# First FFN step of a two-layer block started pair by pair on the modulation chunks

## The chip, the cores and the metric

The kernel runs on one core of one Trainium2 chip. The metric is the device time of one execution in microseconds (us), the median of several runs. The time before is 1221.44 us, the median of 3 runs (1220.31 to 1224.39).

## The reference, cut to what matters

```python
cond = jax.nn.silu(c)                                   # c: (1, 1024)
for l in range(2):
    mod = jnp.einsum('bd,de->be', cond, w_ada[l]) + b_ada[l]      # 1024 x 9216 weights
    sh1, sc1, g1, sh2, sc2, g2, sh3, sc3, g3 = jnp.split(mod, 9, axis=-1)
    h = rms_norm(x, norm_ffn1[l]) * (1 + sc1) + sh1               # x: (256, 1024)
    x = x + 0.5 * g1 * swiglu(h, w_gate1[l], w_up1[l], w_down1[l])   # 1024 x 2816, 2816 x 1024
    h = rms_norm(x, norm_mix[l]) * (1 + sc2) + sh2
    x = x + g2 * token_mixing(h, ...)                             # three kinds of attention
    h = rms_norm(x, norm_ffn2[l]) * (1 + sc3) + sh3
    x = x + 0.5 * g3 * swiglu(h, w_gate2[l], w_up2[l], w_down2[l])
```

All is in f32. Before the first FFN can start, `sh1` and `sc1` must be known: 1024 x 2048 of `w_ada`, 8 MB.

## The kernel before

Everything is written out by hand for each engine: which instruction follows which, and the semaphores between them. Nothing is planned by a scheduler.

**Precision.** A product of f32 values is made of three products of rounded parts: a weight block `raw` (128 x 2048, 1 MB) is turned by ScalarE into `whi` (`split_hi`, line 423) and by VectorE into `wlo = raw - whi` (`split_lo`, line 726). The activations `hTf` (K-tile by token, 128 x 8 x 256) are split in the same way into `hhi` and `hlo`.

**FFN.** `ffn` runs 11 steps of 256 hidden columns. On TensorE (`ffn_step`) a step has 48 gate matmuls, 48 up matmuls (each 128x128 by 128x256) and 24 down matmuls (128x128 by 128x512). The gate product is `by_high` (lines 1129, 1130, then 1133 with `hlo`), the up and down products are `three` (lines 1071 to 1073). VectorE's part of a step begins with `weigh_ada`: two chunks of `w_ada` (for later modulations) are summed over K with silu(c) as factors (lines 682, 684). Only then come the first half of the down block's `wlo` (line 810), the product of silu(gate) and up (815), its low part (817), the second half of `wlo` (819), and the splits of the next gate and up blocks (726). ScalarE makes silu (471), `whi` of the down block, then `guhi` (475) and the next `whi`. The weights are fetched by SyncE's queue (`fill`, line 326), in the order gate, up, down; `w_ada` by GpSimd's queue (lines 385 and 393).

**The start.** `sh1` and `sc1` are the first 2048 columns of `w_ada`, in 8 chunks of 256 columns (1 MB each): chunk m of 0 to 3 holds the shifts of K-tiles 2m and 2m+1, chunk 4+m their scales. All 8 are fetched in order. Chunks 0, 2, 4, 6 go to TensorE (`dot_chunk`, line 1089): each 128x128 piece is the stationary operand and one column of silu(c) the moving one, so that the sums come out as columns, one for each of 128 partitions. Chunks 1, 3, 5, 7 go to VectorE (`weigh_chunk`) and are closed by TensorE with ones (`sum_ada`, line 1080). The first gate and up blocks are requested when chunk 6 has landed. When all 16 columns stand in one bank, `modulation` makes the factors `modA` and `modB` (769, 771), and ScalarE and VectorE put them on while they copy the transposed x out of PSUM (460, 752). ScalarE then makes `hhi` (465) and `split_hi(1, 0)`, VectorE `split_lo(0, 0)`, `hlo` (761) and `split_lo(1, ...)`, and the gate product of step 0 starts.

**Order of the queues.** Each engine takes its instructions strictly in the order written; SyncE's and GpSimd's queues fill in theirs.

Of the kernel before, what the change touches and what calls it, by code (L numbers as in the profile page):

```python
# [15 lines left out]
P = 128  # L16
# [19 lines left out]
def build(nc, x, c, w_ada, b_ada, norm_ffn1, w_gate1, w_up1, w_down1, norm_mix, w_in, qn_a, kn_a, qn_c, kn_c,  # L36
# [36 lines left out]
    ADA_PRE = 1  # L73
# [10 lines left out]
    with ctx:  # L84
# [3 lines left out]
        def sem(name):  # L88
# [63 lines left out]
        pre_ada = [ada[:, 0:1, :, :], ada[:, 1:2, :, :]] + [heads[:, 8 * k:8 * k + 8, :].unsqueeze(1) for k in range(2)] \  # L152
            + [LGs[:, :].rearrange("p (a k n) -> p a k n", a=1, k=KT), hTf[:, :, :].unsqueeze(1)] + [ada[:, 0:1, :, :], ada[:, 1:2, :, :]]
        WEIGHED = (1, 3, 5, 7)
        pre_acc = {1: acc[:, 0:1, :], 3: acc[:, 1:2, :], 5: gate[:, 0:CW].unsqueeze(1), 7: gate[:, CW:2 * CW].unsqueeze(1)}
# [9 lines left out]
        disti, dm4, dm16, strict_i = (eb[:, k * S:(k + 1) * S].bitcast(I32) for k in range(4))  # L165
        upper_i = eb[:, 4 * S:4 * S + P].bitcast(I32)
        distf = xn[:, 0, 0:S]
        ge0 = xn[:, 0, S:2 * S]
        tmpf = xn[:, 0, 2 * S:3 * S]
        maskC = xn[:, 0, 3 * S:4 * S]  # L170
# [3 lines left out]
        GB, UB0, UB1, SB_ = PS[4], PS[5], PS[6], PS[7]  # L174
        PROJ = [PS[0], PS[1], PS[7]]
# [10 lines left out]
        pre_full = [sem(f"pre_full{m}") for m in range(6)]  # L186
# [123 lines left out]
        def _(sp):  # L310
# [40 lines left out]
            sp.wait_ge(ada_full[0], 16)  # L351
            gate_up(0, 0, 0, v_gate, v_up)
# [28 lines left out]
        def _(pool):  # L381
# [30 lines left out]
        def _(act):  # L412
# [21 lines left out]
            def boundary(l, n, x_done):  # L434
# [8 lines left out]
                if l == 0 and n == 0:  # L443
                    split_hi(0, 0)
                high_of_h(l, n)
                if l == 0 and n == 0:
                    split_hi(1, 0)
# [19 lines left out]
            def ffn_step(l, which, i, ahead, after):  # L467
# [3 lines left out]
                act.activation(silu, GB[:, :], ACT.Silu).then_inc(silu_ready, 1)  # L471
# [7 lines left out]
            def ffn(l, which, after):  # L479

                with act.Fori(0, NF - 1) as i:
# [82 lines left out]

            act.wait_ge(tables, 1)
            act.preload_act_table_set("natural_log_exp_and_others")
            for l in range(L):
                boundary(l, 0, nth(l, NB * TT, 0))
# [59 lines left out]
        def _(dve):  # L628
# [8 lines left out]
            for k in range(2):  # L637
                dve.memset(heads1[k * HD:(k + 1) * HD, k * HD:(k + 1) * HD], 1.0)
            dve.wait_ge(iotas, 3)
# [26 lines left out]
            dve.drain()  # L666
            s_a, s_c = slopes()
            for h in range(H_A):
                dve.scalar_tensor_tensor(aliA[:, h, :], distf, -s_a[h], causal[:, :], ALU.mult, ALU.add)
            for h in range(H_C):  # L670
                dve.scalar_tensor_tensor(aliC[:, h, :], distf, -s_c[h], maskC, ALU.mult, ALU.add)
            def late_tables():
                dve.wait_ge(cols_done, 1)
                dve.tensor_copy(cols[:, :, :, :], PS[0][:, 0:L * KT * 13].rearrange("p (l k m) -> p l k m", l=L, k=KT))
                dve.wait_ge(gains_in, 8 * 16)
# [13 lines left out]
            def weigh_chunk(m):  # L689

                dve.wait_ge(pre_full[m] if m < 6 else ada_full[m - 6], 16)
                weigh_rows(pre_acc[m], pre_ada[m])
                if m in (1, 7):
                    dve.drain().then_inc(ada_used[1], 1)
# [51 lines left out]
            def transposed(l, n, gain, shift):  # L746
# [9 lines left out]
                if l == 0 and n == 0:  # L756
                    split_lo(0, 0)
# [697 lines left out]
```

## Time and profile before

| | us |
|---|---|
| median of 3 runs | 1221.44 (1220.31 to 1224.39) |
| the profiled execution, its own time | 1223.01 |
| its span, first to last instruction | 1221.3 |
| TensorE busy | 1163.4 (95%) |
| VectorE busy | 873.8 (72%) |
| ScalarE busy | 530.8 (43%) |
| read from HBM | 256.56 MB, mean 211 GB/s over the span |

The profiled execution took 1223.01 us, 1.7 us more than its span and 1.6 us more than the median. TensorE is busy nearly all the time, so its busy share tells little. What matters for this change is the first 75 us, and there the time at which each piece of work starts.

In the records of the trace, one f32 matmul of the program stands as two records (a chunk's 16 matmuls are 32 records), while a matmul of split parts is one.

### The profile page before, as it was taken

The page shows a single profiled execution, that of the slowest core. Times are in us where ns is not written, and L with a number is a line of the kernel's source. Part 1 is how long each engine was busy: PE and PEld are TensorE (multiplying, and loading weights), DVE is VectorE, ACT ScalarE, POOL GpSimd, SP SyncE. Part 2 cuts the span into 40 slices and gives each one's busy share as a digit, 9 for nine tenths or more (in the row PEclk, how much of TensorE's full clock was granted, in tenths as well). Part 3 has the DMA queues.
Part 4 walks back from the last instruction along what each step waited for, and adds up shares of the span by engine and source line. Part 5 has one row for each costly group of instructions (what it writes and reads, how often), then busy time and mean ns, then how long its engine had stood idle before and what let it go on. Part 6 is the DMA issues. An engine that isn't in the chain of part 4 may idle for free.

```text
span 1221.3 us, 20469 instructions
## 1 busy us (share of the span) xinstructions
PE 1163.4 (95%) x7948; PEld 1070.2 (88%) x7948; DVE 873.8 (72%) x1304; ACT 530.8 (43%) x685; POOL 64.4 (5%) x79
## 2 busy tenths in 40 slices
PE   6899999999998889999989999999999978999998
PEld 6899999989897779999979999998989866999996
DVE  7687888876864786667678887888687577655445
ACT  2244333443566454333453344335256555334432
POOL 2011100100000000000001011100000000000000
PEclk9999999988999889999988999999899978999999
DMA  9788899934510647777756988894633044765561
GB/s 305 247 293 299 302 311 320 319 121 146 166 59 18 234 136 241 249 253 247 250 196 209 329 302 297 298 351 151 204 122 103 6 163 155 246 195 164 169 210 69
DMA packets 160209, 258.24 MB, mean 211 GB/s; under 512 B 8333, under 2 KB 127117, under 8 KB 160159
## 3 DMA queue, kind: packets, MB, share of 16 engines
q1 hardware_dynamic: 140579, 182.12, 45.3%
q0 software_dynamic: 19584, 75.50, 18.4%
q8 instruction: 29, 0.48, 0.2%
q14 instruction: 17, 0.14, 0.0%
HBM read 256.56 MB, written 1.05 MB: 211 GB/s over the span
## 4 chain that ended last, share of the span: by engine, by line
PE 85%; DVE 6%; ACT 5%; DVEq 1%; DMA 1%; issue 1%; ACTq 0%; POOL 0%; POOLq 0%
PE bank L1071 18%; PE bank L1072 18%; PE bank L1073 18%; PE bank L1129 7%; PE bank L1130 7%; PE bank L1133 7%; PE bank L1089 2%; PE bank L1330 1%; DVE wlo L726 1%; PE bank L1249 1%; ACT hhi L465 1%; DMA ada<-in_w_ada_dram 1%; PE bank L1098 1%; ACT whi L423 1%; PE bank L1234 1%
## 5 line engine op out<-in xcount | busy, mean ns | idle before, releaser
L423 ACT ACTIVATE whi<-raw 128x2048 fp32r<-128x2048 f32 (+3 forms) x178 | 323.0, 1818 | 39.8 <-DMA raw<-in_w_gate_dram 11.9
L726 DVE TENSOR_TENSOR wlo<-raw,whi 128x2048 fp32r<-128x2048 f32 (+3 forms) x134 | 283.3, 2144 | 41.9 <-ACT whi L423 40.8
L1071 PE MATMUL bank<-hhi,whi 128*128 128x256 f32 x1008 | 289.9, 288 | 0.0
L1072 PE MATMUL bank<-hlo,whi 128*128 128x256 f32 x1008 | 287.6, 285 | 0.0
L1073 PE MATMUL bank<-hhi,wlo 128*128 128x256 f32 x1008 | 287.5, 285 | 0.0
L1071 PEld LDWEIGHTS bank<-hhi,whi 128*128 128x128 f32 x1008 | 196.2, 195 | 2.3 <-issue 1.8
L1072 PEld LDWEIGHTS bank<-hlo,whi 128*128 128x128 f32 x1008 | 196.0, 194 | 0.5 <-issue 0.5
L1073 PEld LDWEIGHTS bank<-hhi,wlo 128*128 128x128 f32 x1008 | 195.9, 194 | 0.0
L471 ACT ACTIVATE eb<-bank 128x512 f32<-128x512 f32 x44 | 26.3, 597 | 367.0 <-PE bank L1133 367.0
L684 DVE SCALAR_TENSOR_TENSOR room<-ada,cT,room 128x512 f32 (+3 forms) x266 | 170.1, 639 | 20.2
L1129 PE MATMUL bank<-hhi,whi 128*128 128x256 f32 x736 | 184.4, 287 | 0.0
L1130 PE MATMUL bank<-hhi,wlo 128*128 128x256 f32 x736 | 183.8, 286 | 0.0
L810 DVE TENSOR_TENSOR wlo<-raw,whi 128x1024 fp32r<-128x1024 f32 x44 | 53.9, 1224 | 141.6 <-ACT whi L423 141.6
L1130 PEld LDWEIGHTS bank<-hhi,wlo 128*128 128x128 f32 x736 | 143.9, 195 | 1.9
L1129 PEld LDWEIGHTS bank<-hhi,whi 128*128 128x128 f32 x736 | 143.5, 195 | 2.0
L1071 PE MATMUL bank<-whi,guhi 128*128 128x512 f32 x352 | 141.0, 401 | 0.0
L1072 PE MATMUL bank<-wlo,guhi 128*128 128x512 f32 x352 | 139.2, 396 | 0.0
L1073 PE MATMUL bank<-whi,gulo 128*128 128x512 f32 x352 | 139.2, 395 | 0.0
L385 POOL DMA_DIRECT2D ada<-in_w_ada_dram x66 | 58.1, 883 | 984.0 <-DVEq L701 793.4
L1133 PE MATMUL bank<-hlo,whi 128*128 128x256 f32 x736 | 104.8, 286 | 0.0
L1133 PEld LDWEIGHTS bank<-hlo,whi 128*128 128x128 f32 x736 | 96.7, 195 | 0.0
L1073 PEld LDWEIGHTS bank<-whi,gulo 128*128 128x128 f32 x352 | 66.2, 188 | 16.1
(184 smaller groups left out, 1417.3 us busy)
## 6 DMA issues: line engine op xcount, KB each, us to landing
ada<-in_w_ada_dram POOLq DMA_DIRECT2D x68, 1024.0 KB, 5.8
raw<-in_w_gate_dram SPq DMA_DIRECT2D x44, 1024.0 KB, 5.6
raw<-in_w_up_dram SPq DMA_DIRECT2D x44, 1024.0 KB, 7.0
raw<-in_w_down_dram SPq DMA_DIRECT2D x44, 1024.0 KB, 6.5
raw<-in_w_in_dram SPq DMA_DIRECT2D x28, 1024.0 KB, 5.4
raw<-in_w_out_dram SPq DMA_DIRECT2D x8, 512.0 KB, 3.3
raw<-in_w_out_dram SPq DMA_DIRECT2D x4, 1024.0 KB, 4.8
LG<-in_b_ada_dram SPq DMA_DIRECT2D x6, 512.0 KB, 8.3
```

The lines of the kernel that those rows point to most:

```text
L385: pool.dma_start(ada[:, slot, :, :], v_ada[:, row, col]).then_inc(ada_full[slot], 16)
L423: last = act.activation(dst, src, ACT.Copy)
L471: act.activation(silu, GB[:, :], ACT.Silu).then_inc(silu_ready, 1)
L684: last = dve.scalar_tensor_tensor(sums, chunks[:, :, k, :], cT[:, k:k + 1], sums, ALU.mult, ALU.add)
L726: last = dve.tensor_tensor(dst, src, hi.bitcast(F32), ALU.subtract)
L810: dve.tensor_tensor(wlo[2][:, 0:D], raw[2][:, 0:D], whi[2][:, 0:D].bitcast(F32), ALU.subtract)
L1071: pe.matmul(ps, l_hi, r_hi, start=first, stop=False)
L1072: pe.matmul(ps, l_hi, r_lo, start=False, stop=False)
L1073: return pe.matmul(ps, l_lo, r_hi, start=False, stop=last)
L1129: pe.matmul(ps, wh[:, k, :], hhi[:, k, :], start=k == 0, stop=False)
L1130: pe.matmul(ps, wl[:, k, :], hhi[:, k, :], start=False, stop=False)
L1133: last = pe.matmul(ps, wh[:, k, :], hlo[:, k, :], start=False, stop=k == KT - 1)
```

## The change

- GpSimd fetches the 8 chunks in the order 0, 4, 1, 5, 2, 6, 3, 7. Chunk 6 waits for the dot of chunk 0, chunk 3 for that of chunk 4, and chunk 7 for VectorE's sum of chunk 1 (places in SBUF are used again).
- SyncE requests the gate block when chunk 1 (third in the order) has landed and the up block when chunk 3 (seventh) has.
- Six chunks (0, 4, 5, 6, 3, 7) are now TensorE's. In `dot_chunk` silu(c) is the stationary operand (one column), and 256 columns of the chunk stream past it, 8 f32 matmuls for a chunk. The result is a row of one partition; ScalarE copies it (`copy_row`) and TensorE turns it into columns (`turn_row`, two f32 matmuls of one column). VectorE sums chunks 1 and 2.
- The transposed x is copied out plain (ScalarE, four copies). `first_pair(p)` puts the factors of two K-tiles on it and makes `hlo` of them, `first_high(p)` makes `hhi`. `gate_pair(p)` is the quarter of the gate product of step 0 that needs these two K-tiles: 12 matmuls, with one bank for each half of the hidden columns.
- Step 0 of the first FFN is taken out of the loops of TensorE and ScalarE; VectorE's loop is as it was.
- The tables for the position biases (`aliA`, `aliC`, 12 VectorE instructions) are made at the start of token mixing in layer 0.

The core of the diff:

```diff
-            for m in range(6):
-                pool.dma_start(pre_ada[m][:, 0, :, :], v_ada[:, 0:KT, m * CW:(m + 1) * CW]).then_inc(pre_full[m], 16)
-            for k in range(2):
-                fill(k, 1, slice(0, KT), slice((6 + k) * CW, (7 + k) * CW))
+            for m in (0, 4, 1, 5, 2, 6, 3, 7):
+                if m in (6, 3):
+                    pool.wait_ge(row_done, DOTTED.index(0 if m == 6 else 4) + 1)
+                if m == 7:
+                    pool.wait_ge(pre_used, 1)
+                pool.dma_start(pre_ada[m], v_ada[:, 0:KT, m * CW:(m + 1) * CW]).then_inc(pre_full[m], 16)
...
-            sp.wait_ge(ada_full[0], 16)
-            gate_up(0, 0, 0, v_gate, v_up)
+            sp.wait_ge(pre_full[1], 16)
+            fill(0, 0, chunk_cols(raw[0]), v_gate[:, 0:KT, 0:CW])
+            sp.wait_ge(pre_full[3], 16)
+            fill(1, 0, chunk_cols(raw[1]), v_up[:, 0:KT, 0:CW])
...
+            copy_row(4)
+            copy_row(5)
+            first_high(0)
+            split_hi(0, 0)
+            first_high(1)
+            copy_row(6)
+            copy_row(3)
+            first_high(2)
+            copy_row(7)
+            first_high(3)
+            act.sem_inc(hhi_ready, TT)
+            split_hi(1, 0)
...
+            def first_pair(p):
+                ks = slice(2 * p, 2 * p + 2)
+                both = lambda a: a.rearrange("p (m k) -> p m k", m=2)
+                dve.wait_ge(sums_done, p + 1)
+                dve.tensor_tensor(both(modAB[:, :])[:, :, ks], both(PRE_SUMS[p][:, 0:4]), biasL[:, 0:2, ks], ALU.add)
+                dve.drain()
+                dve.scalar_tensor_tensor(modA[:, ks], modA[:, ks], 1.0, colL[:, ks, N_MOD], ALU.add, ALU.mult)
+                dve.drain()
+                dve.wait_ge(raw_h, 2 * TT)
+                for k in (2 * p, 2 * p + 1):
+                    last = dve.tensor_scalar(hTf[:, k, :], hTf[:, k, :], modA[:, k:k + 1], modB[:, k:k + 1], ALU.mult, op1=ALU.add)
+                last.then_inc(first_h, 1)
+                dve.wait_ge(first_hi, p + 1)
+                dve.tensor_tensor(hlo[:, ks, :], hTf[:, ks, :], hhi[:, ks, :].bitcast(F32), ALU.subtract).then_inc(first_lo, 1)
...
+            weigh_chunk(1)
+            first_pair(0)
+            split_lo(0, 0)
+            first_pair(1)
+            weigh_chunk(2)
+            first_pair(2)
+            first_pair(3)
...
             def dot_chunk(m):
+                pe.wait_ge(pre_full[m], 16)
+                n = DOTTED.index(m)
+                if n >= 2:
+                    pe.wait_ge(row_read, n - 1)
+                for k in range(KT):
+                    last = pe.matmul(PRE_ROWS[n % 2][0:1, 0:CW], cT[:, k:k + 1], pre_ada[m][:, k, :], start=k == 0, stop=k == KT - 1)
+                last.then_inc(row_done, 1)
...
+            def gate_pair(p):
+                pe.wait_ge(first_hi, p + 1)
+                if p == 0:
+                    pe.wait_ge(split_done[0], 2)
...
-            last.then_inc(modc_done, 1)
+            dot_chunk(0)
+            turn_h(0, 0)
+            dot_chunk(4)
+            turn_row(0)
+            turn_row(4).then_inc(sums_done, 1)
+            dot_chunk(5)
+            pe.wait_ge(raw_h, 2 * TT)
+            sum_ada(1, [0], PRE_SUMS[1], 0, pre_acc[1])
+            turn_row(5).then_inc(sums_done, 1)
+            gate_pair(0)
+            dot_chunk(6)
+            sum_ada(2, [0], PRE_SUMS[2], 0, pre_acc[2])
+            turn_row(6).then_inc(sums_done, 1)
+            dot_chunk(3)
+            dot_chunk(7)
+            turn_row(3)
+            turn_row(7).then_inc(sums_done, 1)
+            for p in range(1, 4):
+                last = gate_pair(p)
+            last.then_inc(g_done, 1)
```

## Rows read from the trace of the kernel before

**Rows 1.** Timeline, 0 to 75 us, TensorE: start us, us, engine, line, operation, count.
```profile
9.99 6.96 PE L1089 MATMUL bank<-cT,ada 128*128 128x1 f32 x32 [1.05 <-DMA ada<-in_w_ada_dram]
...
52.73 0.64 PE L1129 MATMUL bank<-hhi,whi 128*128 128x256 f32 x1
...
53.38 0.41 PE L1129 MATMUL bank<-hhi,whi 128*128 128x256 f32 x1
53.59 0.41 PE L1130 MATMUL bank<-hhi,wlo 128*128 128x256 f32 x1
...
59.77 1.12 PE L1133 MATMUL bank<-hlo,whi 128*128 128x256 f32 x8
60.73 0.28 PE L1071 MATMUL bank<-hhi,whi 128*128 128x256 f32 x1
...
66.48 0.40 PE L1071 MATMUL bank<-whi,guhi 128*128 128x512 f32 x1
```

**Rows 2.** Chain of waits, 0 to 75 us: start us, us, what.
```profile
2.76 11.75 DMA ada<-in_w_ada_dram
```

**Rows 3.** Issues (GpSimd at 17.25 and 19.70, SyncE at 30.51): KB each, us to landing.
```profile
ada<-in_w_ada_dram POOLq DMA_DIRECT2D x1, 1024.0 KB, 13.2
...
ada<-in_w_ada_dram POOLq DMA_DIRECT2D x1, 1024.0 KB, 13.5
...
raw<-in_w_gate_dram SPq DMA_DIRECT2D x1, 1024.0 KB, 5.7
```

**Rows 4.** Queues, whole span, then 8 to 10 and 17 to 18 us: packets, MB, share.
```profile
q1 hardware_dynamic: 140579, 182.12, 45.3%
...
q0 software_dynamic: 95, 0.39, 53.0%
q1 hardware_dynamic: 96, 0.39, 49.9%
...
q0 software_dynamic: 83, 0.34, 100.0%
q1 hardware_dynamic: 82, 0.00, 6.0%
```

**Rows 5.** Timeline, 36 to 66 us, ScalarE and VectorE.
```profile
36.25 1.91 ACT L423 ACTIVATE whi<-raw 128x2048 fp32r<-128x2048 f32 x1 [11.95 <-DMA raw<-in_w_gate_dram]
...
46.88 0.18 DVE L769 TENSOR_TENSOR modAB<-bank,biasL 128x16 f32<-128x16 f32 x1 [8.55 <-PE bank L1080]
...
48.91 1.06 ACT L465 ACTIVATE hhi<-hTf 128x1024 fp32r<-128x1024 f32 x1
...
54.44 2.28 DVE L726 TENSOR_TENSOR wlo<-raw,whi 128x2048 fp32r<-128x2048 f32 x1
...
57.20 5.71 DVE L684 SCALAR_TENSOR_TENSOR room<-ada,cT,room 128x512 f32 x7
...
63.36 1.23 DVE L810 TENSOR_TENSOR wlo<-raw,whi 128x1024 fp32r<-128x1024 f32 x1 [0.45 <-ACT whi L423]
...
65.40 0.43 DVE L817 TENSOR_TENSOR gulo<-eb,guhi 128x256 fp32r<-128x256 f32 x1 [0.49 <-ACT guhi L475]
```

**Rows 6.** Timeline, TensorE's f32 matmuls at 256 and 370 us.
```profile
256.03 2.73 PE L1098 MATMUL bank<-ones,room 128*128 128x1 f32 x24
...
370.63 0.59 PE L1295 MATMUL bank<-eb,ones 128*128 128x256 f32 x2
371.06 1.02 PE L1296 MATMUL bank<-eb,upper 128*128 128x512 f32 x2
```

**Rows 7.** Busy time by stretch: us, PE, PEld, DVE, ACT, POOL, PEclk, DMA share, GB/s.
```profile
254.00:256.00 2.00, 2.00 (x4) 0.80 (x3) 1.83 (x4) 1.93 (x6) 0.00 (x0) 0.61 0.00 0
...
260.00:262.00 2.00, 2.00 (x11) 2.00 (x11) 2.00 (x6) 0.00 (x0) 0.00 (x0) 0.50 0.33 55
```

**Rows 8.** Timeline, VectorE: the second bias table, and early token mixing.
```profile
10.74 2.76 DVE L671 SCALAR_TENSOR_TENSOR aliC<-xn 128x256 f32<-128x256 f32 x8
...
268.59 2.29 DVE L726 TENSOR_TENSOR wlo<-raw,whi 128x2048 fp32r<-128x2048 f32 x1 [5.92 <-ACT whi L423]
```

More of the change, by code:

```diff
@@ L150, in build @@
         GATE_BIAS = (0, 1, 0)
[L152 to L155, printed above, removed]
+        pre_heads = [heads[:, 8 * k:8 * k + 8, :] for k in range(2)]
+        pre_ada = {0: ada[:, 0, :, :], 4: ada[:, 1, :, :], 1: pre_heads[0], 5: pre_heads[1],
+                   2: LGs[:, :].rearrange("p (k n) -> p k n", k=KT), 6: ada[:, 0, :, :], 3: ada[:, 1, :, :], 7: pre_heads[0]}
+        WEIGHED = (1, 2)
+        DOTTED = (0, 4, 5, 6, 3, 7)
+        pre_acc = {1: acc[:, 0:1, :], 2: acc[:, 1:2, :]}
+        pre_row = lambda m: eb[0:1, 4 * S + DOTTED.index(m) % 2 * CW:4 * S + (DOTTED.index(m) % 2 + 1) * CW]
         rows = vs[0:N_MOD + 4, :, :]
@@ L183, in build @@
         ada_full = [sem(f"ada_full{k}") for k in range(2)]
-        pre_full = [sem(f"pre_full{m}") for m in range(6)]
+        pre_full = {m: sem(f"pre_full{m}") for m in pre_ada}
+        pre_used = sem("pre_used")
+        row_done = sem("row_done")
+        row_read = sem("row_read")
+        raw_h = sem("raw_h")
+        sums_done = sem("sums_done")
+        first_h = sem("first_h")
+        first_hi = sem("first_hi")
+        first_lo = sem("first_lo")
+        gate_first = sem("gate_first")
         ada_used = [sem(f"ada_used{k}") for k in range(2)]
@@ L465, in high_of_h, with ffn_step @@
                     act.activation(hhi[:, :, t * P:(t + 1) * P], hTf[:, :, t * P:(t + 1) * P], ACT.Copy).then_inc(hhi_ready, 1)
-            def ffn_step(l, which, i, ahead, after):
+            def ffn_step(l, which, i, ahead, after, gated=False):
                 base = turn(l, U_FFN[which])
@@ L479, in ffn @@
             def ffn(l, which, after):
-                with act.Fori(0, NF - 1) as i:
+                if l == 0 and which == 0:
+                    ffn_step(l, which, 0, True, turn(l, U_FFN[which] + 1), True)
+                with act.Fori(1 if l == 0 and which == 0 else 0, NF - 1) as i:
                     ffn_step(l, which, i, True, turn(l, U_FFN[which] + 1))
@@ L665, in _, with alibi @@
                 dve.tensor_tensor(maskC, maskC, ge0, ALU.add)
[L666 to L671, printed above, removed]
+            def alibi(which):
+                s_a, s_c = slopes()
+                if which == 0:
+                    for h in range(H_A):
+                        dve.scalar_tensor_tensor(aliA[:, h, :], distf, -s_a[h], causal[:, :], ALU.mult, ALU.add)
+                else:
+                    for h in range(H_C):
+                        dve.scalar_tensor_tensor(aliC[:, h, :], distf, -s_c[h], maskC, ALU.mult, ALU.add)
             def late_tables():
@@ L755, in transposed @@
                     last.then_inc(hTf_ready, 1)
-                if l == 0 and n == 0:
-                    split_lo(0, 0)
                 for t in range(TT):
@@ L982, in _ @@
                         head_norm(l, n - 2)
+                    if l == 0 and n in (0, 1):
+                        alibi(n)
                     if n + 2 < NC:
@@ L1134, in by_high, with ffn_step @@
                 return last
[L1136 removed]
+            def ffn_step(l, which, i, is_last, gated=False):
                 use = i + turn(l, U_FFN[which])
                 n = i + nth(l, 2 * NF, which * NF)
[L1139 to L1143 removed]
+                if not gated:
+                    pe.wait_ge(split_done[0], use + 2)
+                    wh, wl = chunk_cols(whi[0]), chunk_cols(wlo[0])
+                    for ft in range(2):
+                        last = by_high(l, 2 * which, GB[:, ft * S:(ft + 1) * S], wh[:, :, ft * P:(ft + 1) * P], wl[:, :, ft * P:(ft + 1) * P])
+                    last.then_inc(g_done, 1)
                 pe.wait_ge(split_done[1], use + 2)
@@ L1187, in ffn @@
                     pe.matmul(DB[b][:, :], zero16[:, :], zero16[:, :].unsqueeze(1).to_broadcast([P, HALF // P, P]), start=True, stop=False)
-                with pe.Fori(0, NF - 1) as i:
+                if l == 0 and which == 0:
+                    ffn_step(l, which, 0, False, True)
+                with pe.Fori(1 if l == 0 and which == 0 else 0, NF - 1) as i:
                     ffn_step(l, which, i, False)
```

130 lines of the change are left out of this document (73 added, 57 removed).

## Prediction

> **What bounds the kernel now.** I read the page first, for the share of TensorE; then the chain of waits over 0 to 75 us; then the timelines of that stretch, engine by engine; then the landing of each transfer and what each queue moved. The kernel is TensorE's from the first gate matmul on: it starts at 52.73, the gate product ends and the up product starts at 60.73, and the first down matmul starts at 66.48, with no wait between [rows 1]. So the change is worth what it moves that down matmul, as long as the later steps follow one another as before.
>
> Ahead of 52.73 the chain is first a transfer (the second chunk, landed at 2.76 + 11.75 = 14.5 [rows 2]) and then TensorE's own column sums: 6.96 us a chunk [rows 1]. The transfers were done sooner: chunks 6 and 7 landed at 17.25 + 13.2 = 30.5 and 19.70 + 13.5 = 33.2, the gate block at 30.51 + 5.7 = 36.2 [rows 3]. That is (33.2 - 14.5) / 6 = 3.1 us for each MB, the wires being full.
>
> TensorE's clock has to be read from spacings here. Early matmuls 256 columns wide start 0.21 us apart (53.38, 53.59), later ones (1.12 - 0.28) / 7 = 0.12 us [rows 1]: 1.2 and 2.4 GHz. The one-column records start (6.96 - 0.35) / 31 = 0.21 us apart early and (2.73 - 0.25) / 23 = 0.11 us at 256 us [rows 1, 6]. So TensorE, though busy, ran at 1.2 GHz until some 5 us after 52.73.
>
> **Part 1, the dots.** A chunk is now 8 f32 matmuls of 256 columns, two records each. Two such records take 371.06 - 370.63 = 0.43 us at 2.4 GHz [rows 6], so a chunk takes 8 x 0.43 = 3.4 us, and at 1.2 GHz 6.9 us, which is what it takes now. All depends on the clock. For 2.4 GHz speaks that wide f32 matmuls (L1106) brought it up by 256 us (0.61 granted over 254 to 256 [rows 7]); against it that 27 us of one-column products did not. With one stationary column nothing in the trace shows it. I take the wide moving operand as the nearer likeness: 2.4 GHz from about 15 us.
> The Trainium skill, "TensorE: Matmul & The Clock Gate", section "Part 1: The HAM clock gate", says that the throttled state is the default and that activity releases it. The early row does not agree if activity means a busy engine: busy with one-column products it stayed at 1.2 GHz. By the rule the dots cost 3.4 us; by that row 6.9.
>
> **Part 2, TensorE until it must wait.** Dot 0 from 9.99, up to 15 at 1.2 GHz (0.73 of it) and the rest at 2.4: 15.9. The transposes wait for x and VectorE; I put their end at 19.6. Dot 4 ends at 23.0; two turns of rows (two one-column matmuls each, 0.22 us apiece) and a ScalarE copy of some 0.5 (between 0.18 and 1.06 [rows 5]) end at 24.2; dot 5 at 27.6; closing chunk 1's sum and a turn, 28.6. Next in TensorE's order is `gate_pair(0)`, and behind it stand dots 6, 3, 7 and all the other pairs.
>
> **Part 3, the new wait.** `gate_pair(0)` needs the gate block, landed and split. It is requested at the landing of the third chunk, 14.5 + 3.1 = 17.6 (some 18), instead of 30.51. But GpSimd's queue is then full of chunks, and the engines serve the two queues packet by packet: 95 against 96 packets over 8 to 10 us, and 83 against 82 over 17 to 18 us, where one side moved 0.34 MB and the other 0.00 [rows 4]. GpSimd's packets hold 0.39 MB / 95 = 4.1 KB, SyncE's on the whole 182.12 MB / 140579 = 1.3 KB, and those of a block with rows of 1 KB, 1 KB. So the gate block gets one byte in five, about 0.07 of 0.34 MB/us, from 20 us on: 20 + 1.05 / 0.07 = 35. It lands at 35.3, against 36.2 before. This is where the head start goes. Then 1.91 and 2.28 us for its two splits [rows 5] and 0.2 between them: `gate_pair(0)` starts at 39.7, after a wait of 11 us. VectorE's sum of chunk 1 and its other work before this are over by 25 and hide there; ScalarE's are too.
>
> **Part 4, what is queued behind it.** After the wait the clock is 1.2 GHz again, for up to 5 us (as after 52.73). Pair 0: 12 x 0.21 = 2.6, to 42.3. Dot 6: 0.35 of it by 44.7, the rest at 2.4 GHz, 46.9. Sum and turn of chunks 2 and 6 (VectorE's sum of chunk 2 after `first_pair(1)` is ready at about 46.6), 1.2: 48.1. Dots 3 and 7, whose chunks have landed by 37: 6.9, to 55.0. Two turns and a copy, 1.3: the last sums stand at **S = 56.3**. Pairs 1 to 3: 36 x 0.12 = 4.3, gate product done at 60.6. So far it is as before (60.73).
>
> **Part 5, what is late next.** The up product waits for two splits that before were done by 56.7 (54.44 + 2.28 [rows 5]). Now ScalarE's `split_hi(1, 0)` stands behind `first_high(3)`, which stands behind S. From S: two small operations and two multiplications on VectorE 1.2 (from 0.18 and the like), `first_high` 0.6 (half of 1.06), 1.9, 2.3 [rows 5], 0.1: the up product starts at S + 6.1 = 62.4. Behind that same `split_lo` VectorE has, as always, `weigh_ada` ahead of the down block: from 56.64 (0.47, then 5.71 from 57.20) to 62.9, then 63.36 to the end of the first `gulo` at 65.83 [rows 5]. That is 6.3 + 2.5 = 8.8 us that was hidden under 60.73 to 66.48 and now starts at 62.4: the first down matmul at S + 14.9 = **71.2**, against 66.48: 4.7 us later. The next gate block's split follows 2.3 us after the second `gulo`, still under the 5.6 us of down products, so step 1 goes on without a further wait. Between up and down TensorE now waits 3 us; should the clock fall there, as it did after 2.73 us of one-column work at 256 us (granted 0.50 over 260 to 262 [rows 6, 7]), that costs 0 to 1.7 us more.
>
> **Parts at nothing.** The bias tables (2.76 us for eight instructions, so 4.2 for twelve) move into early token mixing, where VectorE waits 5.92 us at once for ScalarE [rows 8]; without that gap they would cost the 4.2. The loops shortened by one step, and the added semaphores, I put at 0, between -0.5 and +0.5.
>
> **Sum.** +4.7 and some 0.3 for the possible fall of the clock: +5.0 on 1223.01, 1228.0 for a profiled execution. That one was 1.6 above the median, so the median is 1221.4 + 5.0 = **1226.4**; with the bounds, 1224.5 to 1229.
>
> **Rivals.** (a) *The clock stays low through the dots.* For it: 27 us of one-column products, and one stationary column is little work; against it: wide f32 matmuls raised it. Dot 0 to 17, transposes 20.5, dot 4 27.4, dot 5 36, pair 0 from 41.4 to 44, dots 6, 3, 7 with sums: S = 44 + 3 x 6.9 + 3 = 67.7. The down matmul comes at S + 14.9 = 82.6: +16, **1237.5**. It decides as soon as a dot takes over some 4 us.
> (b) *The gate block is early.* Were the queues served byte for byte, or SyncE first, it would land at 20 + 6.3 = 26.5; then `split_hi(0, 0)` follows the copy of row 5 and `gate_pair(0)` starts at 32.7, 7 us sooner; chunk 7 lands at 38. S = 48.5 to 49.3, down at 63.3 to 64.2: -2.3 to -3.2, **1218.5**. Against it: [rows 4]. The Trainium skill, "DMA: Bandwidth & Descriptors", section "Queues, rings and completion order", says that an engine takes whole packets from the queues in turn; the trace agrees (95 to 96), and it is against this change.
> (c) *The clock does not fall in the wait, or is back at once*: pair 0 and dot 6 save 1.1 + 1.2, **1224**.
> (d) *A cheaper start than I count* (an engine order that overlaps more, the 8.8 us of VectorE shorter), no mechanism seen: below 1218.
>
> **How the numbers follow.** Forecast 0.50 (1224.5 to 1229), (a) 0.22, (b) 0.12, (c) 0.10, (d) 0.06. 0.3% is 3.7 us, about what can be told from no change. Faster: (d) and half of (b), 0.12. Same: half of (b), most of (c), a little of the forecast's lower end: 0.19. Slower: 0.69. The range 1218 to 1238 takes in all but (d), the lower half of (b) and the upper part of (a).
>
> **What would show it.** The gate block's landing near 35; dots of 3.4 us after the first; a wait of some 11 us before `gate_pair(0)`; up from 62 and down from 71; VectorE's `weigh_ada` starting only with the up product. It is wrong if dots take 6.9 us, if the gate block lands before 30, or if the down product starts before 67.

## The result

The median of five runs of the changed kernel is 1231.3 us (1227.16 to 1235.62), against 1221.44 for the kernel before in the same round: a ratio of 1.0061, with a 95% interval of 1.0032 to 1.0091. It is slower by 7.5 us by the ratio and by 9.9 us by the medians; another round (experiment 12, below) gave 1236.24 us and 1.0109. The forecast was 1226.4 (1224.5 to 1229 if its mechanism held), with a range of 1218 to 1238 over all rivals and "slower" the likeliest. The profiled execution took 1233.36 us with a span of 1231.7, against 1223.01 and 1221.3: 10.4 more. So it shows the loss, and can be read against the kernel before.

The first fence is the TensorE timeline of the changed kernel up to the second step (start, duration, engine and line, operands, count, and in brackets the idle time before it with what ended it). It answers to [rows 1].

```profile
9.91 6.07 PE L1169 MATMUL bank<-ada,cT 128*1 128x256 f32 x16 [0.74 <-DMA ada<-in_w_ada_dram]
...
20.15 3.61 PE L1169 MATMUL bank<-ada,cT 128*1 128x256 f32 x16
...
24.76 3.61 PE L1169 MATMUL bank<-room,cT 128*1 128x256 f32 x16
...
28.84 0.60 PE L1178 MATMUL bank<-ones,eb 1*128 1x1 f32 x4
39.33 0.55 PE L1196 MATMUL bank<-hhi,whi 128*128 128x256 f32 x1 [9.89 <-DVE wlo L800]
...
42.16 3.63 PE L1169 MATMUL bank<-ada,cT 128*1 128x256 f32 x16
...
54.01 1.13 PE L1178 MATMUL bank<-ones,eb 1*128 1x1 f32 x8
55.07 0.39 PE L1196 MATMUL bank<-hhi,whi 128*128 128x256 f32 x1
...
61.25 0.39 PE L1149 MATMUL bank<-hhi,whi 128*128 128x256 f32 x1 [0.72 <-DVE wlo L800]
...
70.14 0.80 PE L1149 MATMUL bank<-whi,guhi 128*128 128x512 f32 x1 [2.88 <-DVE gulo L886]
70.73 0.63 PE L1150 MATMUL bank<-wlo,guhi 128*128 128x512 f32 x1
71.16 0.63 PE L1151 MATMUL bank<-whi,gulo 128*128 128x512 f32 x1
...
76.79 0.40 PE L1150 MATMUL bank<-wlo,guhi 128*128 128x512 f32 x1
77.03 0.40 PE L1151 MATMUL bank<-whi,gulo 128*128 128x512 f32 x1
...
78.66 0.28 PE L1235 MATMUL bank<-hhi,whi 128*128 128x256 f32 x1
```

A chunk's dots take 3.61 us, half of the 6.96 of [rows 1], and the engine still gains nothing, since it then waits 9.89 us for the gate block. The last sums stand at S = 55.1 and the first down matmul starts at 70.14, against 66.48. The down matmuls then start 0.43 us apart (70.73, 71.16) instead of 0.24 (76.79, 77.03, which is the spacing of the kernel before too) until 76.3. The second step's gate product starts at 78.66, against 72.09 before: 6.6 us later.

The second fence is ScalarE and VectorE over the same stretch, which answers to [rows 5].

```profile
34.95 1.91 ACT L439 ACTIVATE whi<-raw 128x2048 fp32r<-128x2048 f32 x1 [5.65 <-DMA raw<-in_w_gate_dram]
36.89 2.29 DVE L800 TENSOR_TENSOR wlo<-raw,whi 128x2048 fp32r<-128x2048 f32 x1 [6.87 <-ACT whi L439]
...
56.97 1.90 ACT L439 ACTIVATE whi<-raw 128x2048 fp32r<-128x2048 f32 x1
58.90 2.29 DVE L800 TENSOR_TENSOR wlo<-raw,whi 128x2048 fp32r<-128x2048 f32 x1 [1.03 <-ACT whi L439]
61.67 5.72 DVE L742 SCALAR_TENSOR_TENSOR room<-ada,cT,room 128x512 f32 x7
...
69.66 0.42 DVE L886 TENSOR_TENSOR gulo<-eb,guhi 128x256 fp32r<-128x256 f32 x1 [0.48 <-ACT guhi L491]
```

The up block's splits run at 56.97 and 58.90, behind S. `weigh_ada` runs behind them, from 61.11 to 67.4, and `gulo` at 69.66 lets the down product go.

The table shows how much later than in the kernel before ScalarE's `silu` comes in its one profiled execution. It comes once in every FFN step, so it tells in which stage time is lost. In these three nothing changes within the first FFN; nearly all that changes does so between FFNs (boundaries and token mixing).

| us against the kernel before | second step | end of FFN 1 | after mixing, layer 0 | before mixing, layer 1 | after it |
|---|---|---|---|---|---|
| changed kernel | +6.58 | +6.58 | +7.15 | +5.90 | +10.30 |
| changed kernel, once more | +4.20 | +4.20 | +8.44 | +8.46 | +12.05 |
| kernel before, once more | -0.10 | -0.10 | -0.15 | -0.15 | -0.12 |

In the first profile two thirds of the loss are made in the first 78 us. Behind them 3.7 us more appear: +0.6 in layer 0's mixing, -1.3 from there to layer 1's, and +4.4 in layer 1's mixing. The second profile of the same kernel has other parts: 4.2, then 4.2 and 3.6 in the two mixings. So a difference of 2 us between two single profiles, at any of these places, is not yet an effect.

### The profile page after: what moved, and what is told of

Its sections match the earlier page's. It is cut to its first block, busy times and chain, and to the rows that moved or that the text cites. A ratio compares the mean times of both kernels' runs of the same rounds, so it can differ in the third digit from the quotient of the medians.

```text
span 1231.7 us, 20425 instructions
## 1 busy us (share of the span) xinstructions
PE 1163.1 (94%) x7932; PEld 1053.3 (86%) x7932; DVE 867.9 (70%) x1296; ACT 532.2 (43%) x690; POOL 64.6 (5%) x79
## 4 chain that ended last, share of the span: by engine, by line
PE 76%; DVE 10%; ACT 5%; DMA 4%; DVEq 2%; issue 2%; ACTq 0%; POOL 0%; POOLq 0%
PE bank L1149 17%; PE bank L1150 17%; PE bank L1151 17%; PE bank L1236 6%; PE bank L1239 6%; PE bank L1235 6%; DVE room L742 2%; DVE wlo L800 2%; DMA ada<-in_w_ada_dram 2%; DMA raw<-in_w_gate_dram 1%; PE bank L1439 1%; PE bank L1358 1%; DMA room<-in_w_ada_dram 1%; ACT whi L439 1%; ACT hhi L477 1%
## 5 line engine op out<-in xcount | busy, mean ns | idle before, releaser
L1149 PEld LDWEIGHTS bank<-hhi,whi 128*128 128x128 f32 x1008 | 196.1, 195 | 4.3 <-issue 2.7
L1235 PEld LDWEIGHTS bank<-hhi,whi 128*128 128x128 f32 x720 | 140.1, 195 | 1.9
L399 POOL DMA_DIRECT2D ada<-in_w_ada_dram x64 | 56.3, 883 | 977.1 <-DVEq L775 813.9
L1149 PEld LDWEIGHTS bank<-whi,guhi 128*128 128x128 f32 x352 | 67.2, 191 | 18.7 <-DVE gulo L886 3.6
```

The lines of the kernel that those rows point to most:

```text
L399: pool.dma_start(ada[:, slot, :, :], v_ada[:, row, col]).then_inc(ada_full[slot], 16)
L1149: pe.matmul(ps, l_hi, r_hi, start=first, stop=False)
L1235: pe.matmul(ps, wh[:, k, :], hhi[:, k, :], start=k == 0, stop=False)
```

## The experiments

The theory: TensorE executes in order, and the gate block, which is late, holds all the sums behind `gate_pair(0)` (**order**); from S on a chain of the up split, `weigh_ada` and `gulo`, hidden before, sets the down product (**chain**); its wait lets the clock fall (**clock**). The rival: the time is lost elsewhere, to the moved tables, the added semaphores or the place of the work in time.

**1. All dots ahead of the gate pairs.** The order alone is turned; nothing is left out.

```diff
             turn_row(5).then_inc(sums_done, 1)
-            gate_pair(0)
             dot_chunk(6)
+            dot_chunk(3)
...
-            for p in range(1, 4):
+            for p in range(4):
```

ScalarE's `split_hi(0, 0)` goes behind the copy of row 6, and VectorE's `split_lo(0, 0)` behind its sum of chunk 2.

> gate_pair(0) no longer stands ahead of the dots on TensorE: order is dots 0, 4, 5, 6, 3, then the sum of chunk 2 and the turn of row 6, dot 7, the last turns, then all four gate pairs; ScalarE's split_hi(0, 0) moves behind the copy of row 6, VectorE's sum of chunk 2 ahead of split_lo(0, 0). Everything is still computed. My theory (the changed kernel loses its time because the late gate block, landed at 34.9, stops TensorE ahead of dots 6, 3, 7, and all that follows hangs on the last sums S = 55.1): the dots run as their chunks land, dot 7 ends near 41.5, S near 43, the up product starts near 49 and the first down matmul near 58, i.e. 12 us before the changed kernel's 70.1 and 8 us before the kernel before's 66.5; step 1 starts 6 us or so before that of the kernel before if the clock falls again in the wait ahead of down. Time about 0.995 of before. Rival theory (the chunks themselves, or VectorE's chain, bound S whatever TensorE's order): S stays above 50 and the time stays within 2 us of the changed kernel.

Measured: 1220.58 us, ratio 0.998 (0.9955 to 1.0005). The gate pairs start at 44.51 with no wait, up at 51.04, down at 59.58, and the second step comes 5.25 us sooner than in the kernel before, 11.8 sooner than in the changed one. The order theory holds: the place of `gate_pair(0)`, with the two splits that follow it, was worth 10.6 us at the down matmul (9.5 against the second profile of the changed kernel, which has it at 69.03).

```profile
43.44 1.13 PE L1178 MATMUL bank<-ones,eb 1*128 1x1 f32 x8
44.51 0.39 PE L1196 MATMUL bank<-hhi,whi 128*128 128x256 f32 x1
...
51.04 0.47 PE L1149 MATMUL bank<-hhi,whi 128*128 128x256 f32 x1
...
59.58 0.50 PE L1149 MATMUL bank<-whi,guhi 128*128 128x512 f32 x1 [2.44 <-DVE gulo L886]
```

But in time the gain is 2.6 us and not sure to differ from none: layer 1's token mixing gave 9.9 us back in its profile (-8.03 before it, +1.83 behind). That execution took 1224.87 us, 4.3 more than the median of its ten, so the usual one gives back less.

**2. The gate block as the fifth transfer of GpSimd's queue**, so that no queue stands against it.

```diff
             for m in (0, 4, 1, 5, 2, 6, 3, 7):
...
+                if m == 5:
+                    pool.dma_start(chunk_cols(raw[0]), v_gate[:, 0:KT, 0:CW]).then_inc(gate_first, 16)
```

> The order on all engines as in the changed kernel; only the first gate block is fetched by GpSimd's queue, fifth after chunks 0, 4, 1, 5, instead of by SyncE's. Theory that the two queues are served packet by packet, so that the gate block in 1 KB packets was starved beside the 4 KB packets of the chunks: it now lands in its turn, near 24.5, each later chunk 3.1 us later than now; gate_pair(0) starts near 33.7 instead of 39.3, S near 49.5, down near 64.5: 5.6 us less than the changed kernel, near 1.000 of before with the clock falls it keeps. Rival theory (the gate block was late because it was requested late or because the wires were full): it lands after 30 and the time is that of the changed kernel.

Measured: 1229.24 us, ratio 1.005 (1.0019 to 1.0081). The block landed at 24.3, before ScalarE could take it at 28.7, and `gate_pair(0)` began at 33.1 after 4.1 us, the splits' own time. Down starts at 63.93, and the second step 7.6 us sooner than in the changed kernel. So the lateness of the block is most of the wait. Why it is late isn't shown by this run, since the edit also brings the request forward, from 18.1 to 5.5 us. In the whole time no gain is shown: the ratio is 1.005 against 1.0061 for the changed kernel, and their intervals overlap.

**3. 26 matmuls of no use in the wait before the first down product**, to keep the clock up.

```diff
+                if gated:
+                    pe.wait_ge(silu_ready, 1)
+                    for k in range(26):
+                        pe.matmul(SB_[:, 0:S], hhi[:, k % KT, 0:P], hhi[:, k % KT, :], start=True, stop=True)
                 pe.wait_ge(gulo_ready, n * 2 + 1)
```

> The changed kernel plus 26 matmuls of 256 columns into a free bank, between the up and the down product of step 0, where TensorE waits 3.2 us (67.0 to 70.1) for gulo; their result is not used. They take 26 x 0.12 = 3.1 us. Theory that this wait lets the clock fall to 1.2 GHz and that the fall costs 2.9 us (14 down matmuls 0.43 us apart instead of 0.23): down still starts near 70.2, all its matmuls are 0.23 apart, step 1 starts 2.9 us sooner, at +3.7 instead of +6.6 against the kernel before. Rival theory (the slow down matmuls come from something else, such as the banks or weights read late): they stay 0.43 apart and the time is that of the changed kernel.

Measured: 1228.9 us, ratio 1.0065 (1.0043 to 1.0088).

```profile
68.01 3.28 PE L1274 MATMUL bank<-hhi 128*128 128x256 f32 x26
71.13 0.42 PE L1149 MATMUL bank<-whi,guhi 128*128 128x512 f32 x1
71.38 0.40 PE L1150 MATMUL bank<-wlo,guhi 128*128 128x512 f32 x1
71.62 0.39 PE L1151 MATMUL bank<-whi,gulo 128*128 128x512 f32 x1
```

The down matmuls now start 0.24 us apart at once. Down began 1.0 us later than in the changed kernel (its whole start was 0.9 later), and the second step still came 1.9 sooner: 2.9 us, all of the slow matmuls' price. The clock theory holds for the place; the whole time shows no gain (1.0065 against 1.0061).

**4. `weigh_ada` of the first step at its end**, so that it doesn't stand ahead of `gulo`.

```diff
+                if late:
+                    weigh_ada([i + ada_turn(l, k, 1) for k in range(2)], [0, 1],
+                              held[:, at_cols(i * (2 * CW), 2 * CW)].rearrange("p (a n) -> p a n", a=2))
```

> VectorE's step 0 is taken out of its loop and its weigh_ada (6.3 us) stands at the end of the step instead of at its head; all else as in the changed kernel, everything is computed. Theory that this sum, which starts only with the up product, makes the wait ahead of down: the first gulo is ready before the up product ends, down starts at 67.0 to 67.2 without a wait and at 2.4 GHz, and step 1 starts near 72.7, at +0.6 against the kernel before instead of +6.6; at most 1.6 us come back in step 1, where VectorE has two sums in a row. Time about 1.001 to 1.002 of before. Rival theory (ScalarE's whi of the down block or its own copies set the wait): down stays near 70 and nothing is gained.

Measured: 1244.61 us, ratio 1.0197 (1.0153 to 1.024). The second step came at +1.23, as expected; the third at +16.5, which was not.

```profile
89.43 0.48 DVE L740 TENSOR_SCALAR room<-ada,cT 128x512 f32 x1 [9.57 <-DMA ada<-in_w_ada_dram]
...
97.97 0.42 DVE L888 TENSOR_TENSOR gulo<-eb,guhi 128x256 fp32r<-128x256 f32 x1 [0.48 <-ACT guhi L491]
```

The slots that `weigh_ada` reads came free some 13 us later, so the next chunks were requested later, and VectorE waited 9.57 us for them ahead of the second step's `gulo`. The chain theory is right about what holds `gulo`: the first one ran at 66.02 instead of 69.66. Moving the sum only shifted the wait to a transfer.

**5. Both: the order of 1, and the up block's splits ahead of the last sums.**

```diff
             first_high(2)
+            split_hi(1, 0)
             copy_row(7)
...
             first_pair(2)
+            split_lo(1, 0)
             first_pair(3)
```

> e1_dots_first plus the up block's two splits put ahead of the last sums: ScalarE's split_hi(1, 0) ahead of the copy of row 7, VectorE's split_lo(1, 0) ahead of first_pair(3). Everything is computed. Theory (in the changed kernel and in e1 the chain behind the last sums S, namely up split, then the 6.3 us of weigh_ada, then gulo, decides when down starts): the up block landed near 40, so its splits end by S = 44.5; weigh_ada starts at S + 2.5 instead of S + 6.1; pairs and up product end at S + 11.6 = 56.1, gulo is ready at 55.9, and down starts at 56.2 (e1: 59.6) without a wait, so the clock stays at 2.4 GHz. Step 1 starts near -10.5 us against the kernel before (e1: -5.3, the changed kernel +6.6). Time about 0.992 of before. Rival theory (in step 0 something else, such as whi of the down block, comes last): step 1 starts within 1 us of e1's.

Measured: 1219.03 us (12 runs) against 1223.35, ratio 0.9957 (0.9931 to 0.9982): faster than both kernels.

```profile
42.90 0.60 PE L1180 MATMUL bank<-ones,eb 1*128 1x1 f32 x4 [1.15 <-ACT eb L588]
...
57.30 0.50 PE L1151 MATMUL bank<-whi,guhi 128*128 128x512 f32 x1 [1.24 <-DVE gulo L886]
57.63 0.40 PE L1152 MATMUL bank<-wlo,guhi 128*128 128x512 f32 x1
```

`weigh_ada` now starts at 48.26 and down at 57.30, the clock stays up (57.63 and on, 0.24 apart), and the second step is 9.08 us ahead of the kernel before. The cost of the move is the 1.15 us in which row 7's copy stands behind `split_hi`. The whole time shows 5.3 us of the 9.1. The profiled execution, with 1226.88 us, is 7.9 slower than the median of the twelve, so what its stages lose behind the first FFN isn't the usual.

**6. The up block's splits alone moved**, the order of the changed kernel kept: the splits' diff of 5.

> The changed kernel with only that move: ScalarE's split_hi(1, 0) ahead of the copy of row 7, VectorE's split_lo(1, 0) ahead of first_pair(3), both in time that these engines wait in. gate_pair(0) stays ahead of the dots, S stays near 55.1. Same theory: the up product follows the gate product (up at 60.5), weigh_ada starts near 57.7, gulo is ready near 66.5, down starts at 66.5 with no wait to speak of and at 2.4 GHz; step 1 starts at 72.3, at +0.1 to +0.6 against the kernel before instead of +6.6. So of the 6.6 us, all but those would be the chain behind S with its clock fall. Rival theory (the late gate block alone makes the loss): step 1 stays above +5.

Measured: 1228.73 us, ratio 1.0052 (1.0028 to 1.0075). The second step came at -2.14, far sooner than expected, but two things had changed: the gate block landed at 30.0 and `gate_pair(0)` began at 35.56, 3.8 us sooner than in the changed kernel. The wait before down was 1.09 instead of 2.88, and the fall of the clock went. That leaves some 2 us for the splits and 2.9 for the clock, as a split of one profile against one and not isolated. The edit touches nothing that runs before 30 us, so the earlier landing is not its doing. What differed in this execution is dot 4 (28.84 and 20.15 in the changed kernel are here 30.83 and 21.36):

```profile
17.81 1.11 PE L1224 MATMUL bank<-ident,xn 128*128 128x128 f32 x8 [3.10 <-DVE xn L816]
...
21.36 4.39 PE L1171 MATMUL bank<-ada,cT 128*1 128x256 f32 x16
...
30.83 0.38 PE L1180 MATMUL bank<-ones,eb 1*128 1x1 f32 x2
```

Dot 0 had ended 1.3 us earlier (14.7 for 16.0) and the normalised x came 0.4 us later, so that TensorE waited 3.10 us for it instead of 1.46. What followed went in part at the lower clock: the second four transposes took 1.94 us for 1.11, and dot 4 took 4.39 for 3.61 and ended 2.0 us later. With it came GpSimd's next request, which waits for dot 4: at 26.05, against 24.06. What that does to the gate block stands below.

**7. The eight loads of the head gains behind the gate block.** They are tiny (elements of 4 bytes), and stand ahead of the gate block on SyncE's queue in both kernels.

```diff
-            for n, g in enumerate((qn_a, kn_a, qn_c, kn_c)):
-                for half in range(2):
-                    sp.dma_start(qkg[half * HD:half * HD + HD, :, n], g.rearrange("l p -> p l"),
...
             fill(0, 0, chunk_cols(raw[0]), v_gate[:, 0:KT, 0:CW])
+            (the same lines)
```

> The changed kernel with the eight small loads of the head gains (1024 packets of 4 bytes in the trace) requested behind the first gate block on SyncE's queue instead of ahead of it. The trace of the changed kernel shows them served one for one with GpSimd's 4 KB packets until 24.6, and the gate block's own packets only from 24.6 on, done but for a few per cent by 29; the last of these trickle, 5 a microsecond, until 34.9. Theory A (the queue ahead of the block is what delays it): the block starts to flow near 20 and lands by 28 to 29, gate_pair(0) starts near 33.5 instead of 39.3, S near 50, step 1 starts 5 us sooner than in the changed kernel, at +1 to +2. Theory B (it is its 1 KB packets beside 4 KB ones that are starved as long as GpSimd's queue has work, whatever stands ahead): it lands at 33 or later and the time is that of the changed kernel.

Measured: 1235.37 us (4 runs), ratio 1.0099 (1.0062 to 1.0137). `gate_pair(0)` began at 35.26, 4.1 us sooner, and the second step 5.0 sooner (+1.58), of which 1.3 are a shorter stretch of low clock. Against the second profile of the changed kernel (37.35 and +4.20) they came 2.1 and 2.6 us sooner. This is how the two queues stand over 22 to 23 us:

```profile
q0 software_dynamic: 68, 0.28, 80.9%
q1 hardware_dynamic: 68, 0.07, 23.4%
```

The 68 packets of SyncE's queue are now the gate block's, where in the changed kernel they were tiny ones. It went on like this from some 21.4 to 25 us, so about a quarter of the block went in that time. So the tiny loads are a part of the block's lateness. The whole time doesn't show the gain: 1.0099 against 1.0061 and 1.0109 for the changed kernel in its two rounds. The profiled execution, 1228.56 us, is the fastest of the four and 6.8 below their median.

**8 to 12. The time behind the first FFN.** Since the whole time did not follow the second step, the kernel before was run unchanged (8), and with 24, 40 and 64 matmuls of no use ahead of its first FFN loop (9 to 11), so that all of it comes later and nothing else differs; the changed kernel was run once more (12).

```diff
+                if l == 0 and which == 0:
+                    for k in range(24):
+                        pe.matmul(SB_[:, 0:S], hhi[:, k % KT, 0:P], hhi[:, k % KT, :], start=True, stop=True)
                 with pe.Fori(0, NF - 1) as i:
```

> The kernel before as it was, for a second profile. The changed kernel's profile is 6.6 us behind that of before from step 1 to the end of the first FFN and 10.4 at the end, with 4.4 of it gained in the second layer's token mixing. If that is the fall and rise of TensorE's clock in the places where it waits, which differ from one execution to the next, two profiles of the same kernel agree to 0.1 us up to the end of the first FFN and then drift apart by 1 to 5 us in the same places. If it is the change, they agree to 1 us to the end.

> The kernel before with nothing of the change, but with 24 added matmuls of 256 columns (into a free bank, result unused) right ahead of the first FFN loop on TensorE, so that all that follows is shifted: by 24 x 0.21 = 5.1 us less 2.2 us for the 24 slow matmuls of the gate product that now run at 2.4 GHz, +2.9 us at step 1. Theory P (the places where TensorE's clock falls and rises depend on when a stage comes, so a pure shift changes what they cost): the whole time differs from before by 2.9 us plus something of its own, between -3 and +8 us, and the profile shows the difference arise in the boundaries and in token mixing. Theory Q (what the changed kernel and the experiments lose behind the first FFN is a cost of the change, such as the tables made in token mixing): the whole time is that of before plus 2.9, within 1 us.

> The same with 40 added matmuls: +2.9 + 16 x 0.12 = +4.8 us at step 1. Theory P: the whole time is before + 4.8 plus something that is not that of the run with 24 (they differ by over 2 us in it). Theory Q: before + 4.8, within 1 us.

> The same with 64 added matmuls: +7.7 us at step 1, about what the changed kernel has there (+6.6). Theory P: before + 7.7 plus something of its own. Theory Q: before + 7.7, within 1 us, and more than the changed kernel by 1.

> The changed kernel as it was, beside the shifted ones on one chip, with a second profile. Up to the end of the first FFN it agrees with the first profile to 0.2 us (+6.6 at step 1 against the kernel before). The time is 1.006 of before, within 0.003. If the losses behind the first FFN are the same in both profiles (10.3 at the last FFN), they are fixed by when the stages come; if they are not, they differ from one execution to the next.

| run | median us, against | ratio (95%) | second step | before mixing, layer 1 | after it |
|---|---|---|---|---|---|
| 8, before again | 1223.58 (one run) | | -0.10 | -0.15 | -0.12 |
| 9, +24 | 1225.57, 1224.57 | 1.0023 (0.9986 to 1.0059) | -0.61 | -0.67 | +0.91 |
| 10, +40 | 1228.56, 1224.57 | 1.0044 (1.0006 to 1.0083) | +5.26 | +4.44 | +5.90 |
| 11, +64 | 1230.72, 1224.57 | 1.0047 (1.0009 to 1.0085) | +8.14 | +7.53 | +11.24 |
| 12, changed again | 1236.24, 1224.57 | 1.0109 (1.0075 to 1.0144) | +4.20 | +8.46 | +12.05 |

The pure shifts of 10 and 11 arrive in the whole time as 5.4 and 5.8 us: a shift is carried on roughly as it is, with 2 to 4 us either way. The profile of run 9 has -0.61 instead of +2.9, and its TensorE rows tell why. These are the transposes and the last one-column dot, ahead of all that was added, first of run 9 and then the dot of the kernel before:

```profile
35.71 3.65 PE L1116 MATMUL bank<-ident,xn 128*128 128x128 f32 x16
39.16 3.97 PE L1089 MATMUL bank<-cT,ada 128*128 128x1 f32 x32
```

```profile
39.09 6.83 PE L1089 MATMUL bank<-cT,ada 128*128 128x1 f32 x32
```

In that execution the clock rose soon after the start of this dot, which took 2.9 us less, and everything behind came 3.1 us sooner. So also the kernel before doesn't always start its gate product at 52.7. By the ratio over its ten runs, run 9 is 2.8 us slower (by the medians 1.0), for 2.9 expected.

Run 8 missed its expectation, a drift of 1 to 5 us between two profiles of one kernel: they agree within 0.15 us to the end. Run 12 missed its own too. It is the same kernel as the changed one, yet its gate pair began at 37.35 and not 39.33, and mixing cost it 4.2 and 3.6 us where the first profile shows 0.6 and 4.4. So one execution of a kernel is no measure of those stages.

The clock differs there. In layer 0's mixing run 12 was granted 0.64, 0.50 and 0.50 over the 30 us from 384.2, where the first profile has 1.00, 0.66 and 0.66 over the same stretch of work, from 386.6. For layer 1, these are the same 20 us of the execution (us, busy time of PE, PEld, DVE, ACT and POOL, granted clock, DMA share, GB/s), first of the kernel before:

```profile
970.00:980.00 10.00, 7.63 (x67) 7.26 (x66) 4.34 (x11) 7.80 (x22) 0.00 (x0) 0.96 0.18 54
980.00:990.00 10.00, 5.01 (x20) 3.81 (x20) 8.06 (x26) 6.59 (x21) 0.00 (x0) 0.67 0.30 99
```

and of experiment 1, which arrived there 8 us early:

```profile
970.00:980.00 10.00, 9.31 (x45) 8.91 (x44) 2.15 (x5) 4.84 (x13) 0.00 (x0) 0.50 0.16 52
980.00:990.00 10.00, 5.62 (x23) 4.58 (x23) 7.88 (x27) 6.49 (x24) 0.00 (x0) 0.50 0.17 48
```

At 0.50 TensorE is busier with fewer matmuls (9.31 us for 45, against 7.63 for 67). The work in the two windows isn't quite the same, as experiment 1 came 8 us early. The same 16 matmuls, one stage of this mixing, compare cleanly, first of the kernel before, then of experiment 1:

```profile
976.37 2.00 PE L1330 MATMUL bank<-room,pT 128*128 128x64 f32 x16 [0.74 <-ACT pT L547]
```

```profile
977.46 3.67 PE L1439 MATMUL bank<-room,pT 128*128 128x64 f32 x16 [0.69 <-ACT pT L565]
```

So a stage that goes at one clock in one execution can go at the other in the next. That fits the 9.9 us which experiment 1 lost in that mixing; it wasn't made to vary by itself.

**What stays open.** The changed kernel and every experiment made from it end later than their second step says: by the ratio less the second step, +0.9 (changed), 2.8, 3.3 and 3.8 (experiments 1, 3, 5), and 7 to 11 us (2, 4 from its third step, 6, 7 and 12), where the shifts 10 and 11 give +0.1 and -2.4, and 9 gives -0.1 if the 2.9 us of its added matmuls are taken for the shift (+3.4 with its profile's step). The intervals of these ratios reach 3 to 5 us to either side. The changed kernel itself stands at both 0.9 and 9.1, so the spread is no property of an edit. That pure shifts bring no such loss, as far as their intervals tell, speaks against the mere time of the stages as its cause. Whether the change has a cost of its own in the mixing (the bias tables are there now) or the clock happens to fall worse for these orders, no run separates.

## Why the prediction was right, and where it was off

The direction and the chain up to the down matmul came as put. The size of the time is in part luck of a wide range: 1231.3 lies above the 1224.5 to 1229 that the mechanism gave, between it and rival (a)'s 1237.5, whose mechanism did not occur. Of the 5.0 us forecast and the 7.5 (by the ratio) to 9.9 (by the medians) measured, the difference is a mis-sized fall of the clock and a part behind the first FFN that was not in the sum.

**The dots** came as put: 3.6 us a chunk at 2.4 GHz, the first at 6.07 with its later matmuls already faster. Rival (a) is refuted by the 3.61: the clock rose while dot 0 ran, with one stationary column and 256 moving, where in the kernel before it stayed at 1.2 GHz through four dots, 27 us in all, of one moving column [rows 1]. The rule of the Trainium skill ("TensorE: Matmul & The Clock Gate", "Part 1: The HAM clock gate"), that activity releases the throttle, agrees with the new form. With the old one it doesn't, if a busy engine is activity: there the clock rose during the dots in one of five profiles only, in the last dot, behind 3.65 us of transposes (run 9).

**The wait**: 9.9 us where 11 were put, S = 55.1 for 56.3, up at 61.25 for 62.4, down at 70.14 for 71.2; the shift of the down matmul is 3.7 for 4.7. S + 6.1 and S + 14.9 came as 6.2 and 15.0, instruction by instruction, since all their durations stood in [rows 5].

**The gate block's landing** was right in size (34.9 for 35.3; 33.0 in the second profile) and wrong in mechanism, so the size was luck. I had it flow at a fifth of the bandwidth from 20 us on, which never happened in the changed kernel. Experiment 7 shows that flow, 68 packets and 0.07 MB in a microsecond, once the tiny loads are out of the way. The queues of the changed kernel (packets, MB, share of 16 engines), over 22 to 23, 25 to 26 and 31 to 32 us, show three stages:

```profile
q0 software_dynamic: 90, 0.34, 101.3%
q1 hardware_dynamic: 89, 0.00, 6.5%
...
q1 hardware_dynamic: 305, 0.28, 86.3%
q0 software_dynamic: 23, 0.06, 18.6%
...
q0 software_dynamic: 93, 0.34, 101.8%
q1 hardware_dynamic: 4, 0.00, 1.3%
```

From its request at 18.1 until 24.6 almost nothing of the block moved: SyncE's queue had a packet in turn for each of GpSimd's, but they were the 4-byte packets of the head gains, standing ahead of it. [rows 4] has them (82 packets, 0.00 MB), and I read that row only for the turns and not for what was queued. Then GpSimd's queue ran dry, since its next request waits for dot 4, and the block went nearly alone at 0.28 to 0.33 MB in a microsecond until 28. From 29 on it had 4 or 5 packets a microsecond against 84 to 93, where equal turns on all engines would give 90: the last 2% took until 34.9. The trace's records of single packets tell more. From 29.01 to 34.00, 22 of the block's 1 KB packets start every 0.235 us, 0.052 us long each; one packet of GpSimd's queue takes about 0.18 (1.018 x 16 / 93). So this is the pace of one engine that takes the two queues in turn: the other engines' shares were through, and one was 22 packets behind. That it was one engine is inferred from the pace, since the records don't name it. Experiment 7 bears on the first stage (2.1 to 4.1 us off `gate_pair(0)`), experiment 2 shows that the block can be there by 24.3. How long the third stage is goes with the second: in experiments 1 and 6, where GpSimd's request came at 26.1, the block landed at 30.4 and 30.0. There the last packets came 0.045 to 0.048 us apart, before GpSimd's had come back to the engines that were behind. In the changed kernel (both times) and experiments 3, 4 and 5, with the request at 24.1 or a little sooner, it landed at 33.0 to 35.3. So in these seven executions a later dot 4 goes with an earlier landing; no edit was made for it. The rule of the Trainium skill ("DMA: Bandwidth & Descriptors", "Queues, rings and completion order"), whole packets in turn, agrees with 90 to 89.

**Mis-sized: the fall of the clock before down**, a term of 0 to 1.7 us. It cost 2.9 us in the first profile, shown by experiment 3: 14 matmuls, 0.2 us dearer each. In experiments 1, 7 and 12 a wait of the same kind cost 1.6 to 1.7 (-6.90 at down and -5.25 at the second step in experiment 1), and in experiment 5 a wait of 1.24 us cost nothing. With 3.7 for the down matmul in place of 4.7 the sum of the first step is 6.6 for my 5.0; in the second profile it is 2.6 and 1.6, so 4.2.

**Rivals (b) and (c)**: (b)'s landing, 26.5, was reached in no run that left the gate block on SyncE's queue; on GpSimd's, requested at 5.5 us, it landed at 24.3 (experiment 2). (c) has its half: after the long wait, pair 0 went at 1.2 GHz, but dot 6 began at 42.16 already at the higher level (3.63 us, for my 4.6), which is the microsecond that S is better by.

**Bias tables at nothing** [rows 8]: they run at 267.4 and 271.3, 1.42 and 2.77 us, and layer 0's mixing is 0.6 us longer in one profile and 4.2 in the other. Nothing is shown for a cost or against it.

**Not foreseen**: the 3.7 us (7.9 in run 12) behind the first FFN, nearly as much as the forecast itself. I had carried the first step's loss to the end as it was. For a pure shift experiments 10 and 11 bear that out within 3 us; for this kernel the term needed a spread of several.

## What to carry to other kernels

Where an engine executes in order, put a piece that waits for a late transfer behind all the work whose data are already there, even if the piece came "first" by its dependencies: here it was about 10 us at the down matmul. Before you pull a transfer forward, list what stands ahead of it on its own queue and count packets rather than bytes; and before you move sums later, list what the other engines had hidden behind them. A gain of a few microseconds at the start of a kernel is shown at its place by the trace, but whether it reaches the end has to be measured over many runs.

## What the runs showed of the hardware

- Eight loads of 4-byte elements held their queue against one of 4 KB packets for over 6 us (259 packets each over 17 to 20 us: 1.00 MB against 0.00), one packet for one.
- The last 22 packets of the gate block went one every 0.235 us for 5 us, the pace of one engine that takes a packet from either queue in turn. With the other queue's request 2 us later the block landed at 30.0 and 30.4 instead of 33.0 to 35.3 (seven executions, not isolated by an edit).
- A wait of 2.4 to 2.9 us of TensorE before the first down product was followed by dense matmuls at 1.2 GHz for 3 to 6 us; after one of 1.09 or 1.24 us there were none.
- Dots with one moving column ran at 1.2 GHz, 27 us of them, in four of five profiles of that start; in the fifth (run 9) the last dot took 3.97 us instead of 6.83, behind 3.65 us of transposes. The same sums with the column stationary had the clock up in the first chunk in all nine profiles.
- Two profiled executions of the kernel before agree within 0.15 us in every stage; two of the changed kernel differ by 2.4 us at the second step and by 3.7 in layer 0's mixing.
